# Hybrid streaming encoder step: the attention mask added to the bias by GpSimd, values one unit later, and all token tiles turned beside the conditioning

## The reference

```python
mod = silu(c) @ w_ada + b_ada                      # six parts of 1024: shift, scale, gate, twice
h = rms_norm(x, g_norm1) * (1 + sc1) + sh1
z = h @ w_in                                       # q_a, k_a, v_a, q_idx, k_idx, w_idx, q_b, k_b, v_b, gates
# branch A, sparse attention, 8 heads with one shared key and value row per token
score = sum_h w_idx[h] * relu(q_idx[h] . k_idx)    # causal by chunks of 64
idx = top_k(score, 256)
y_a = softmax(q_a . k_a[idx] / 8 + bias) @ v_a[idx]
# branch B, window attention, 8 heads, 2 key heads, with sinks
x += gt1 * (sigmoid(gate_a) * (y_a @ w_oa) + sigmoid(gate_b) * (y_b @ w_ob)) @ w_out
x += gt2 * relu(h2 @ w_up) ** 2 @ w_down ;  final rms_norm
```

## Time and profile before

| | us |
|---|---|
| median of 3 runs | 1890.08 (1889.33 to 1890.46) |
| the profiled execution | 1900.68 |
| its span | 1898.7 |
| TensorE busy | 1814.7 (96%) |
| VectorE busy | 948.2 (50%) |
| ScalarE busy | 637.0 (34%) |
| GpSimd busy | 465.7 (25%) |
| mean granted TensorE clock | 0.977 |

### The profile page before, as it was taken

One profiled execution on the slowest core, in us unless ns is written; L12 is line 12 of the kernel. 1 busy time (PEld: TensorE's weight loads), 2 busy tenths in 40 slices (PEclk: granted clock), 3 DMA queues, 4 the chain that ended last, 5 costly groups with the idle time before them and its releaser, 6 DMA issues.

```text
span 1898.7 us, 30260 instructions
## 1 busy us (share of the span) xinstructions
PE 1814.7 (96%) x11176; PEld 1721.8 (91%) x11176; DVE 948.2 (50%) x2302; ACT 637.0 (34%) x1237; POOL 465.7 (25%) x269
## 2 busy tenths in 40 slices
PE   7799999999989998999999999999999999999996
PEld 2688999999978887777999999999999999999996
DVE  1657888899155555456564453232323232323234
ACT  3445566641244444444231240313121212121222
POOL 0521222223210001111223222322222222222220
PEclk9899999999998998999999999999999999999998
DMA  7510223242342223664334111111111111111112
GB/s 270 166 48 23 69 85 117 89 133 82 115 109 59 51 65 78 165 166 137 115 115 149 44 41 38 44 45 44 44 44 44 44 44 44 44 44 35 43 44 94
DMA packets 179321, 153.47 MB, mean 81 GB/s; under 512 B 20240, under 2 KB 162016, under 8 KB 178688
## 3 DMA queue, kind: packets, MB, share of 16 engines
q1 hardware_dynamic: 175328, 137.31, 25.2%
q10 hardware_dynamic: 3920, 15.19, 2.0%
HBM read 127.34 MB, written 25.19 MB: 80 GB/s over the span
## 4 chain that ended last, share of the span: by engine, by line
PE 85%; DVE 6%; ACT 4%; DMA 3%; issue 2%; POOL 1%; SPq 0%; DVEq 0%; ACTq 0%; POOLq 0%
PE psum L788 66%; PE psum L1063 5%; PE psum L1054 3%; PE psum L1081 2%; PE psum L912 2%; PE psum L945 2%; PE psum L1026 1%; PE psum L1027 1%; PE psum L826 1%; DVE h_f L1557 1%; PE psum L1030 1%; DVE u_lo L1927 1%; DMA out<-y_out 1%; DMA ada_c<-in_w_ada 1%; DVE score L1614 1%
## 5 line engine op out<-in xcount | busy, mean ns | idle before, releaser
L788 PE MATMUL psum<-h_hi,w_hi 128*128 128x362 f32 (+2 forms) x1440 | 474.5, 330 | 2.5 <-DVE h_lo L1905 1.6
L788 PE MATMUL psum<-h_lo,w_hi 128*128 128x362 f32 (+2 forms) x1440 | 474.0, 329 | 0.0
L788 PE MATMUL psum<-h_hi,w_lo 128*128 128x362 f32 (+2 forms) x1440 | 473.4, 329 | 0.0
L729 POOL CAST w_hi<-w_raw 128x1024 fp32r<-128x1024 f32 x112 | 120.3, 1074 | 1038.8 <-PEq L792 882.6
L731 POOL TENSOR_TENSOR w_lo<-w_raw,w_hi 128x1024 fp32r<-128x1024 f32 x112 | 281.7, 2516 | 9.0
L788 PEld LDWEIGHTS psum<-h_hi,w_hi 128*128 128x128 f32 x1440 | 271.1, 188 | 3.3 <-DVE h_lo L1905 1.9
L788 PEld LDWEIGHTS psum<-h_lo,w_hi 128*128 128x128 f32 x1440 | 271.5, 189 | 0.0
L788 PEld LDWEIGHTS psum<-h_hi,w_lo 128*128 128x128 f32 x1440 | 271.3, 188 | 0.0
L1889 DVE SCALAR_TENSOR_TENSOR xT<-psum,modT,xT 128x364 f32<-128x364 f32 (+3 forms) x288 | 136.1, 497 | 265.6 <-PE psum L788 265.6
L788 PE MATMUL psum<-u_hi,w_hi 128*128 128x362 f32 (+1 forms) x768 | 253.4, 330 | 3.2 <-DVE u_lo L1927 3.2
L788 PE MATMUL psum<-u_lo,w_hi 128*128 128x362 f32 (+1 forms) x768 | 252.0, 328 | 0.0
(11 more groups left out here) (284 smaller groups left out, 2854.4 us busy)
## 6 DMA issues: line engine op xcount, KB each, us to landing
w_raw<-in_w_in SPq DMA_DIRECT2D x32, 512.0 KB, 4.1
ada_c<-in_w_ada SPq DMA_DIRECT2D x32, 512.0 KB, 4.0
w_raw<-in_w_up SPq DMA_DIRECT2D x32, 512.0 KB, 4.1
w_raw<-in_w_down SPq DMA_DIRECT2D x32, 512.0 KB, 3.4
zT_scratch<-z_out ACTq DMA_DIRECT2D x27, 544.0 KB, 3.6
q_raw<-zT_scratch SPq DMA_DIRECT2D x32, 272.0 KB, 5.1
...
```

The costliest lines, as they stand in the source:

```text
L729: pl.tensor_copy(w_hi[slot][:, :], w_raw[slot][:, :]).then_inc(sem("w_hi_made"), 1)
L788: ins = pe.matmul(bank(b, n), w[:, k, wc], x[:, a, c0:c0 + n], start=(m == 0 and p == 0), stop=(m == len(wk) - 1 and p == 2))
```

## The change

In branch A the products with `selmask` and with the diagonal tile are gone from TensorE. GpSimd scales `selmask` once (`scale_mask`), bars the future half block of the bias (`bar_future`), and adds mask and bias per piece into one of two buffers `bias_m`, at most two masked pieces ahead of VectorE (`mask_bias`; `mask_sample` in place for the sample's bias). Its splits of the next pair's queries take fixed places among these. The values of unit n are multiplied in iteration n+1, with four `probT` buffers; the sample unit keeps its own iteration. The outputs of the first three pairs are transposed through free columns of banks 6 and 7 instead of 4 and 5. To make rows of query and mask agree without the reversing product, index queries are written in reversed order, and their weights are reversed by one product (`w_rev`). The load of the third head's queries moves ahead of a wait.

In the head all nine x tiles have their own buffer and are loaded early; they are turned, stored and scaled in groups of one, two, three and three between the four `ada` products. The vectors are loaded and turned before the bias table. The index projections start after six scaled tiles are turned and alternate with the last three, and the cache's transposes come after them.

The diff, cut to its core:

```diff
-        probT = [at(f"probT{s}", [P, 4 * P], F32, B + 15168 + 512 * s) for s in range(2)]
+        bias_m = [at(f"bias_m{s}", [P, 1024], F32, z_out_at + 1024 * s) for s in range(2)]
+        probT = [at(f"probT{s}", [P, 4 * P], F32, B + (15168, 15680, 14016, 14528)[s]) for s in range(4)]
...
+        def weighed_at(n):
+
+            last = units[n - 1] if n else None
+            out = [last] if last and n != NA and (last["br"] == "b" or last["blk"] is not None) else []
+            if n < NA and units[n]["blk"] is None:
+                out.append(units[n])
+            return out
+
+        def slot_of(g, before):
+
+            return g % 2 + 2 * (before % 2) if g < a_groups else g % 2
 
...
+        masked = {}
+        masked_pieces = []
+        for u in units[:NA]:
+            if u["blk"] is not None and u["blk"] >= 2:
+                for piece, _, _ in u["pieces"]:
+                    masked[piece] = len(masked_pieces)
+                    masked_pieces.append(piece)
...
+        XTURNS = [[0], [1, 2], [3, 4, 5], [6, 7, 8]]
+        IDX_BANKS = {(0, 0): 6, (1, 0): 7, (0, 1): 0, (1, 1): 1, (0, 2): 4, (1, 2): 5}
...
-            for n in range(4):
-                load_x(n)
-                if n >= 2:
-                    sp.wait_ge(sem("ada_used"), n - 1)
-                load_ada(n, n % 2)
-                if n >= 2:
-                    store_xT(n - 2)
+            load_x(0)
+            load_ada(0, 0)
+            for t in range(1, 5):
+                load_x(t)
+            load_ada(1, 1)
+            for t in range(5, NT):
+                load_x(t)
...
             load_tile(T_KI, 0)
-            for t in range(4, XRING):
-                load_x(t)
             load_tile(T_QI, 1)
-            for t in range(2, NT):
+            for n in range(2, 4):
+                store_xT(2 * n - 4)
+                store_xT(2 * n - 3)
+                sp.wait_ge(sem("ada_used"), n - 1)
+                load_ada(n, n % 2)
+            for t in range(4, NT):
                 store_xT(t)
-                if XRING <= t + 4 < NT:
-                    load_x(t + 4)
...
+            load_q(2)
...
+            def scale_mask(c, name, rows_ready):
+
+                pl.wait_ge(sem("w_split"), 2 + jobs.n)
+                pl.wait_ge(sem("selected"), NSEL)
+                if rows_ready:
+                    pl.wait_ge(sem("mask_ready"), 1)
+                pl.tensor_scalar(selmask[:, c], selmask[:, c], -NEG_R, None, ALU.mult).then_inc(sem("mask_scaled"), 1)
+                pl.wait_ge(sem("mask_scaled"), name)
+
+            split(0)
+            scale_mask(slice(0, SEL_SAMPLE), 1, False)
+            split(1)
+            scale_mask(slice(SEL_SAMPLE, SEL_W), 2, True)
+
+            def split_q(hh):
+
...
+            def bar_future(pair, half):
+
+                pl.wait_ge(sem(f"biasA_in{half}"), 16 * (pair + 1))
+                pl.memset(biasA[half][64:P, SEQ - CHUNK:SEQ], NEG).then_inc(sem(f"biasA_ready{half}"), 1)
+                pl.wait_ge(sem(f"biasA_ready{half}"), pair + 1)
...
+            def mask_bias(u):
+
+                for piece, c0, w in u["pieces"]:
+                    k = masked[piece]
+                    if k >= 2:
+                        pl.wait_ge(sem("piece_biased"), masked_pieces[k - 2] + 1)
+                    m0 = SEL_OFF[u["blk"]]
+                    for lane, h in enumerate(u["heads"]):
+                        c = lane_at(u, lane)
+                        ins = pl.tensor_tensor(bias_m[k % 2][:, c:c + w], biasA[h % 2][:, SEQ - w:SEQ],
+                                               selmask[:, m0:m0 + w], ALU.add)
+                    ins.then_inc(sem("bias_masked"), 1)
+                    made.next()
...
+            def mask_sample(pair, half):
+
+                c = (slice(0, 1056), slice(1056, SKEYS))[half]
+                pl.wait_ge(sem("biasS_in"), 32 * (pair + 1))
+                pl.tensor_tensor(biasS[:, c], biasS[:, c], selmask[:, SEL_SAMPLE + c.start:SEL_SAMPLE + c.stop], ALU.add)\
+                    .then_inc(sem("biasS_masked"), 1)
...
+            for slot in range(2):
+                pl.wait_ge(sem(f"z_stored{slot}"), 16 * 15)
+            split_after = {starts[hh // 2 - 1] + 7 + 3 * (hh % 2): hh for hh in range(2, 10)}
+            for u in units[:NA]:
+                m = u["n"] - starts[u["pair"]]
+                if m in (0, 4):
+                    if u["n"]:
+                        pl.wait_ge(sem("bias_masked"), made.n)
+                    bar_future(u["pair"], m // 4)
+                if m in (4, 5):
+                    mask_sample(u["pair"], m - 4)
+                if u["blk"] is not None and u["blk"] >= 2:
+                    mask_bias(u)
+                if u["n"] in split_after:
+                    pl.wait_ge(sem("bias_masked"), made.n)
+                    split_q(split_after[u["n"]])
+            for hh in range(10, 16):
+                split_q(hh)
...
-            for n in range(AHEAD):
-                turn_x(n)
+            for n, turns in enumerate(XTURNS):
+                for t in turns:
+                    turn_x(t)
+                if n == 1:
+                    pe.wait_ge(sem("rel_copied"), 1)
                 ada(n, 16 * (n // 2 + 1), n % 2)
...
+            def index_steps(u, g, ks):
+
+                c0, n = GROUPS[g]
+                for k in ks:
+                    if k == 0:
+                        if g == 0:
+                            start_job()
+                        pe.wait_ge(sem("bank_free"), uses.next())
+                        pe.wait_ge(sem("h_lo_done"), -(-(c0 + n) // P))
+                    for p, (w, x) in enumerate(((w_hi, h_hi), (w_hi, h_lo), (w_lo, h_hi))):
+                        ins = pe.matmul(bank(IDX_BANKS[u, g], n), w[u][:, k * P:k * P + P], x[:, k, c0:c0 + n],
+                                        start=(k == 0 and p == 0), stop=(k == KT - 1 and p == 2))
+                    if k == 0 and (u, g) in ((0, 0), (1, 2)):
+                        pe.wait_ge(sem("acc_full"), uses.n)
+                        pe.sem_inc(sem("w_used"), 1)
+                if k == KT - 1:
+                    ins.then_inc(sem("acc_full"), 1)
+
+            for t in range(6):
+                turn_normed(t)
             pe.wait_ge(sem("xT_staged"), NT)
...
+            turn_normed(6)
+            index_steps(0, 0, range(4, KT))
+            turn_normed(7)
+            index_steps(1, 0, range(KT))
+            turn_normed(8)
+            for g in (1, 2):
+                for u in range(2):
+                    index_steps(u, g, range(KT))
+
...
-                            masked = u["br"] == "a" and (u["blk"] is None or u["blk"] >= 2)
-                            diag = u["br"] == "a" and not masked and cc + n == w
                             pe.matmul(out, q, khi, start=True, stop=False)
-                            ins = pe.matmul(out, q, klo, start=False, stop=not (masked or diag))
-                            if masked:
-                                m0 = (SEL_SAMPLE if u["blk"] is None else SEL_OFF[u["blk"]]) + c0 + cc
-                                ins = pe.matmul(out, swap_r[:, :], selmask[:, m0:m0 + n], start=False, stop=True)
-                            if diag:
-                                ins = pe.matmul(psum_w[:, out0 + w - P:out0 + w], swap_r[:, :], diag_r[:, :],
-                                                start=False, stop=True)
+                            ins = pe.matmul(out, q, klo, start=False, stop=True)
...
-                    ins = pe.matmul(bank(6 + u["n"] % 2)[:, HD * lane:HD * lane + HD], probT[s][0:n, m * P:m * P + P],
+                    ins = pe.matmul(bank(6 + u["n"] % 2)[:, HD * lane:HD * lane + HD], probT[slot_of(g, before)][0:n, m * P:m * P + P],
...
+            def turn_outputs_a(n, pair, part):
+
+                pe.wait_ge(sem("y_done"), n - 1)
+                for m, t in enumerate(units[starts[pair + 1] - 1]["turn"][part][1]):
+                    w = P if t < NBLK else DEC
+                    ins = pe.transpose(bank(6 + n % 2)[:, (m + 1) * P:(m + 1) * P + w], y_tok[pair_slot(pair)][0:w, t, :],
+                                       ident[0:w, 0:w])
+                ins.then_inc(sem("y_turned"), 1)
+
...
-                if 1 <= u["n"] <= 4:
-                    pe.wait_ge(sem("kAS_lo_done"), u["n"])
+                for pair, part in turned_after(u["n"]):
+                    if pair < 3:
+                        pe.wait_ge(sem("y_turn_read"), 3 * pair + part + 1)
...
                 for pair, part in turned_after(n):
-                    turn_outputs(pair, part)
+                    if pair < 3:
+                        turn_outputs_a(n, pair, part)
+                for past in weighed_at(n):
+                    weigh_all(past)
+                for pair, part in turned_after(n):
+                    if pair >= 3:
+                        turn_outputs(pair, part)
...
-            for n in range(AHEAD):
-                x_stats(n)
+            for n, turns in enumerate(XTURNS):
```

(28 more changed lines are left out.)

237 lines of the change are left out of this document (135 added, 102 removed).

## The result

The changed kernel takes 1882.3 us (median of 6 runs, 1880.65 to 1883.57) against 1890.27 for the kernel before beside it (6 runs, 1888.68 to 1900.01): ratio 0.9949, 95% interval 0.9929 to 0.9969. (A ratio here is estimated from all executions, so it differs a little from that of the two medians, 0.9958.) A second set (the fifth experiment) gave 0.9926, 0.9903 to 0.9949. The forecast of 1856 us had the sign right and was 26 us off, outside its range of 1838 to 1876. One execution of all those reported, of run 6 at a mean clock of 0.84, took 1982.67 us and is left out of that run's figures. The profiled execution took 1881.54 us, its span 1879.7, at a mean granted clock of 0.98.

What follows compares the result with a forecast made beforehand. PE was taken to bound the projections and branch A's pairs (46.3 us work, 9.9 waits and lower clock). Terms -30.7 - 10.5 + 5.0 + 2 = -34.2 gave 1866 profiled, 1856 us median; range 1838 to 1876.

Steps and rivals of the forecast that it cites:

- the same difference from that gives 1856: Final conversion: profiled execution lay 10.6 us above the 1890.08 median, so 1866 for a profiled run became 1856.
- Masks off PE, -5.4 a pair: Branch A: 29 mask products a pair leave PE, all on the path, saving 5.4 us a pair.
- The waits that go, 5 us a pair left: Branch A: later values and separate output turns leave 5 us of waits a pair where 9.9 were (bounds 1.5 and 9.9).
- own bank for output turns: Branch A: output turns avoid the transpose banks, so yA_lo waits, two of about 1 us at every pair's start, go.
- The sum of 46: Branch A pair: 46.3 of work - 5.4 masks + 5 waits = 45.9 us, against 56.2; pairs 2 to 4 save 30.7.
- Lower clock goes with the waits: Branch A: stretches at 1.2 GHz, costing up to 6.8 us a pair, follow the yA_lo waits and mostly go with them.
- GpSimd, 31 us a pair at 2.3 ns a column, off the path: Branch A: GpSimd's mask additions and splits take 31 us of a 46 us pair, so its throughput is not the bound.
- Rival (c): Branch A: POOL additions run 1.83 times as long beside DVE, 57 us a pair, so 1907 us, slower; chance 0.04.
- The start, +5.0: Start of branch A: DVE's first unit waits for POOL's first mask, until about 524.7 instead of 519.74: +5.0 us (bounds +3, +8).
- The head, +2: Head: first h_f near 68 instead of 55.76, mostly paid back, first index score at 117.5: +2 us (bounds -5, +6).
- rival (d): Head: work beside the conditioning costs more than is repaid, +12 with clock down, branch A as forecast: 1866 us; chance 0.07.
- (a): Branch A: waits and lower clock keep their 9.9 us a pair, mainly the masks' 21.6 saved: 1869 us; chance 0.17.

Runs made afterwards that it cites:

- the fifth experiment: The changed kernel, no edit, run again on another chip beside the kernel before: 1880.06 us, ratio 0.9926.
- run 6: Changed kernel with two orders swapped in the first three output turns (ScalarE: yA_hi before next query; VectorE: y_tok before yA_lo): 1870.91 us, ratio 0.9887.
- experiment 1: The kernel before, no edit, profiled and timed again: median 1893.85 us, ratio 0.9987; profiled execution 1893.54.
- 10: Changed kernel with the two output-chain swaps, but masks of upper blocks and sample added by TensorE again (25 products a pair): 1879.52 us, ratio 0.9936.
- 7: Changed kernel with values multiplied in their own iteration again, as before the change: 1891.05 us, ratio 0.9981 to the kernel before.
- 11: Changed kernel with values in their own iteration and the two output-chain swaps: 1885.4 us, ratio 0.9959 to the kernel before.
- 12: Changed kernel with the two output-chain swaps and the selection mask left out of branch A, for timing only: 1869.94 us, ratio 0.9881.
- 4: Changed kernel with GpSimd's masks of the first two units put between the first and second query's splits: 1878.76 us, ratio 0.9906.
- 3: Changed kernel with SyncE's queue reordered in the head (third ada block, xT stores as staged, last x tiles behind): 1874.67 us, ratio 0.9891.
- 8: Changed kernel with the head of the kernel before, the first two masks earlier and the two output-chain swaps: 1862.05 us, ratio 0.9829.
- 9: Changed kernel with its head requeued and x turns alternating over two PSUM bank pairs, plus early first masks and output-chain swaps: 1861.08 us, ratio 0.9830.

## Why the prediction was wrong

By its own steps.

- **"the same difference from that gives 1856"** failed: 11 us. The sum was made against an execution that lay 10.6 us above the median, and the forecast took that excess off as if it would be in the changed kernel too; the changed kernel's profiled execution lies 0.8 below its median. Of the excess, 5.7 us are seen as lower-clock time in the pairs (1). Against experiment 1's profile the three pairs save 15.8 us instead of 21.5. Those terms had to be made against pairs of 54.1 us, or the excess taken off the gain.
- **Masks off PE, -5.4 a pair**: the work is as counted (4.6 us busy for 25 of the 29 products, 4.9 worked out), but for those a pair gets shorter by 3.4 only (10 against 6), since other waits take part of it.
- **The waits that go, 5 us a pair left**: "own bank for output turns", by which "the yA_lo waits go", was the step that failed. The wait went from the transposes, but the chain behind it stayed, queued behind exponentials, a query conversion and, on VectorE, the next y_tok. The forecast named blocks 2 and 3 and the sample unit as late next; it was the turned outputs again. Three pairs saved 21.5 us, not 30.7; freeing that chain in 6 gave the missing 9.2. The sum of 46 was right there for a pair without it, its split was not: work had been put at 40.9 and waits at 5, and run 6 shows 42.7 busy and 3.2 waiting at clock 1.00.
- **Lower clock goes with the waits**: borne out in part. With the chain freed it was gone in all fifteen pairs (6), though waits of up to 1.1 us stayed. The sum of the waits doesn't decide it: in 7 and 11 four of six pairs ran at 1.00 with 5.7 to 6.4 us of waits. Nor is it fixed: experiment 1 has it in one pair and not in the next, with the same instructions and waits for yA_lo of 2.1 and 2.6 us.
- **GpSimd, 31 us a pair at 2.3 ns a column, off the path**: right for the pairs, by the profile and by 12. Rival (c), contention, didn't occur. In branch A the rule of the Trainium skill on it ("GPSIMD Engine Reference", 8. Key points: contention with VectorE instructions that have two SBUF inputs) wasn't tested, since VectorE's large operations read PSUM there.
- **The start, +5.0**: right for VectorE. 4 shows that an earlier first mask alone gives only 1.5 us of it back.
- **The head, +2**: failed, +7.8 measured; rival (d) had the place right and +12. From the first h_f on all went as worked out (48.3 us to the first index score, 49.5 forecast). The error is before it: 74.88 instead of 68. The waits on the shared bank pair were in the sum; 1.7 us stood for stores that hold the staging buffers and for the clock together. The stores alone made ScalarE wait 9.2 us, of which 3.6 showed in the end (3), and the third and fourth products lost 1.8 and 2.6 us against the second, at granted clocks of 0.79 and 0.72. Together that is 8.0 us where 1.7 stood, and the first h_f came 6.9 us late.

Of the rivals, (a) came nearest, waits and lower clock that stay, though in part only: a pair of 48.9 us has 8.0 beyond the 40.9 of work, where (a) had 9.9 and the forecast 5. No rival had the possibility that the baseline's own excess was counted as gain and then taken off again.

The change itself is worth 8 to 14 us by the medians of the two sets; the kernels of 8 and 9, which keep its branch A and mend the orders around it, are 1.7% below the kernel before.
